# Splitting the tail of an output projection over POOL, ACT and DVE in an encoder layer

## The chip, the cores and the metric

The kernel runs on one core of one Trainium2 chip. The metric is the device time of one execution in microseconds (us), lower is better. The engines are named as in the profile: PE (TensorE, matrix products and transposes), DVE (VectorE), ACT (ScalarE), POOL (GpSimd) and SP (SyncE, which here only issues transfers). Each engine takes its own instructions in program order; between engines only semaphores set an order.

## The reference

One layer of a bidirectional encoder with adaLN conditioning is applied to two groups of tokens, 256 "prompt" and 1024 "sample" tokens of width 1024, that share all weights. All inputs and outputs are float32. Per layer:

```
h  = RMSNorm(x) * (1 + scale1) + shift1
q, k, v, gates of two attention branches = h @ w_in
x  = x + gate1 * ((sigmoid(gA) * oA + sigmoid(gB) * oB) @ w_out)
h2 = RMSNorm(x) * (1 + scale2) + shift2
aff = softmax(h2 @ w_router); each of 16 experts takes its top 2n/16 tokens
x  = x + gate2 * (weighted sum of expert SwiGLU outputs)
y  = RMSNorm(x)
```

The case is about the third to fifth line: the residual, the second norm and its modulation by scale2 and shift2, and the router behind them. The modulated h2 is transposed (features on partitions), so scale and shift are one number per partition there. The experts' token lists need the router values of all tokens of a group.

## The kernel before

The 1280 tokens are 10 tiles of 128 (NT = 10; tiles 0 and 1 are the prompt). `plan_steps` writes out one list of steps by hand, and every engine walks through this same list and issues its own part of each step. For the stage in question the list is a loop over t from 0 to 12, and each pass holds, in this order:

- `O` t: PE multiplies tile t of the merged attention output with w_out, 48 products of 128 x 512 in bf16 into two PSUM banks (lines 1376 to 1378). It waits for `out_free`, so that the banks of two tiles before are read.
- `X2` t-1: PE transposes the normalised tile `xn2` in two halves of four transposes (line 1431) and DVE modulates each transposed 128 x 128 block (`modulate`, line 1029), eight per tile, into `h2T`.
- `RT` t-2: PE computes the router logits of a tile in 16 products (line 1591), DVE takes the row maximum (line 1236), ACT the exponential (line 945), DVE reciprocal and scaling (lines 1238 and 1239).
- `AT` t-3: PE transposes the affinities (line 1597), DVE copies them out (line 1247).
- `K` 0, in pass 6 only: DVE picks the prompt's top tokens (`topk`, lines 1037 to 1044).
- `XO` t: DVE waits for `out_done` and multiplies the projection in PSUM with gate1 (line 1225), adds the residual `xo` (line 1227), waits for ACT's sum of squares (line 939), scales it (1019), waits for ACT's square root (941), takes the reciprocal (1021) and scales the rows into `xn2` (1229). POOL then stores `xn2` and `x1` to DRAM (lines 672 and 673).

Behind the loop come the diagonals of gate2 (`GT` 4 to 7, lines 1205 and 1529), the sample group's top 128 tokens (`K` 1, 48 long DVE instructions), the transposes of the lists (`I`), and then the gather of the first expert's tokens and the experts. `XO` t is the last step of pass t, while the transposes that read its `xn2` are in pass t+1, behind the products of tile t+1. ACT's square root and its exponential need different tables, so that a table load (`ACT_TABLE_LOAD`) stands before each of them.

The ring of three PSUM banks for transposes (`job_at`, `t_free`) is freed by whoever read a bank. Line numbers below are those of the printed kernel.

Of the kernel before, what the change touches and what calls it, by code (L numbers as in the profile page):

```python
# [19 lines left out]
ALU = mybir.AluOpType  # L20
ACT = mybir.ActivationFunctionType
AX = mybir.AxisListType

P = 128
D = 1024
# [3 lines left out]
NT = TOK // P  # L29
# [12 lines left out]
EPS = 1e-6  # L42
# [33 lines left out]
def group_of(t):  # L76
    return 0 if t < PT_TILES else 1
# [120 lines left out]
def encoder(nc, x_p, x_s, c_p, c_s, w_ada, b_ada, n1g, w_in, qg, kg, sink, w_ba, w_bb, w_out, n2g, w_router,  # L198
# [25 lines left out]
    with ExitStack() as ctx:  # L224
# [3 lines left out]
        def sem(name):  # L228
            return ctx.enter_context(nc.semaphore(name))
# [62 lines left out]
        xo = at(12288, 2, D)  # L292
        x1 = at(14336, 2, D)
        xn2 = at(16384, 2, D)
        h2T = [at(18432, KD, P), at(46592, KD, P)]
# [24 lines left out]
        modT = sb("modT", [P, 48, 2])  # L320
        A1 = sb("A1", [P, KD, 2])
        A2 = sb("A2", [P, KD, 2])
# [9 lines left out]
        rs = sb("rs", [P, 2, 8])  # L332
# [33 lines left out]
        ssq = sem("ssq")  # L366
        rms_in, rms_sqrt = sem("rms_in"), sem("rms_sqrt")
# [11 lines left out]
        msum, mhigh = sem("msum"), sem("mhigh")  # L379
        wos_hi, wos_ready = sem("wos_hi"), sem("wos_ready")  # L380
        out_done, out_free = sem("out_done"), sem("out_free")
        xo_in = [sem("xo_in0"), sem("xo_in1")]
        x1_ready, xn2_ready = sem("x1_ready"), sem("xn2_ready")
        x1_out, xn2_out = [sem("x1_out0"), sem("x1_out1")], [sem("xn2_out0"), sem("xn2_out1")]
# [226 lines left out]
        def _(gp):  # L611
# [12 lines left out]
            for s in steps:  # L624
                k = s[0]
                if k == "RB":
                    g = s[1]
                    if g:
                        gp.wait_ge(t_done, job_at[(("OT", g - 1), 0)] + 1)
                    if NPAIR * g == first_b:  # L630
                        gp.wait_ge(pv_done, first_b)
                    gp.wait_ge(rinv_ready, g + 1)
                    gp.tensor_tensor(rb_of(g).rearrange("p (h d) -> p h d", d=HD),  # L633
                                     ones[:, 0:HD].unsqueeze(1).to_broadcast([P, 8, HD]),
                                     rinv[:, g % 2].unsqueeze(2).to_broadcast([P, 8, HD]), ALU.mult).then_inc(rb_ready, 1)
                if k == "NM":
                    g = s[1]
                    br, _, qt, _ = items[NPAIR * g]
                    o = oT[:, NPAIR * br:NPAIR * br + NPAIR, qt]
                    src = on_of(g).rearrange("p (j q) -> p j q", j=NPAIR)  # L640
                    gp.wait_ge(o_norm, g + 1)
                    gp.tensor_tensor(o[:, :, 0:P], src, ones[:, 0:NPAIR].unsqueeze(2).to_broadcast([P, NPAIR, P]), ALU.mult)\
                        .then_inc(o_high, 1)
                    gp.wait_ge(o_high, g + 1)
                    gp.tensor_tensor(o[:, :, P:2 * P], src, o[:, :, 0:P], ALU.subtract).then_inc(o_split, 1)
                if k == "HS":

                    t = s[1]
                    if t == 0:
                        gp.wait_ge(t_done, job_at[(("AR", 11), 0)] + 1)  # L650
                        gp.wait_ge(pv_done, first_b)
                    a, z = t * P, t * P + P
                    gp.tensor_tensor(hTs[:, 0:KD, a:z], hT[:, :, a:z], ones[:, 0:KD].unsqueeze(2).to_broadcast([P, KD, P]),
                                     ALU.mult).then_inc(hs_hi, 1)
                    gp.wait_ge(hs_hi, t + 1)
                    gp.tensor_tensor(hTs[:, KD:2 * KD, a:z], hT[:, :, a:z], hTs[:, 0:KD, a:z], ALU.subtract).then_inc(hs_done, 1)
                if k == "M":
                    n = (s[1] * 3 + s[2])
                    w = 256 if s[2] == 2 else 512
                    gp.wait_ge(mm_ready, n + 1)  # L660
                    tmp = sig[:, n % 2, 0, 0:w]
                    cols = slice(s[2] * 512, s[2] * 512 + w)
                    gp.tensor_tensor(tmp, tmp, sig[:, n % 2, 1, 0:w], ALU.add).then_inc(msum, 1)  # L663
                    gp.wait_ge(msum, n + 1)
                    gp.tensor_tensor(mergedS[:, s[1], cols], tmp, ones[:, 0:1].to_broadcast([P, w]), ALU.mult).then_inc(mhigh, 1)
                    gp.wait_ge(mhigh, n + 1)
                    gp.tensor_tensor(mergedS[:, KD + s[1], cols], tmp, mergedS[:, s[1], cols], ALU.subtract)\
                        .then_inc(merged_ready, 1)
                if k in ("XO",):
                    t = s[1]  # L670
                    gp.wait_ge(xn2_ready, t + 1)
                    gp.dma_start(token_rows(xn_d, t), xn2[:, t % 2]).then_inc(xn2_out[t % 2], 16)
                    gp.dma_start(token_rows(acc_d, t), x1[:, t % 2]).then_inc(x1_out[t % 2], 16)
# [96 lines left out]
        def _(ac):  # L770
# [23 lines left out]
            for s in steps:  # L794
                k = s[0]
                if k == "vec":
                    b, free = job(s)
# [4 lines left out]
                if k == "br":  # L802
                    b, free = job(s)

                    ac.activation(brow[:, s[1], :], b[:, 0:RELW], ACT.Copy).then_inc(brow_ready, 1)
                if k == "AR":
                    c = s[1]
                    b, free = job(s)
# [4 lines left out]
                if k == "XP":  # L813
                    t = s[1]
# [7 lines left out]
                if k == "G":  # L822
                    t = s[1]
# [4 lines left out]
                    for c in range(3):  # L828
                        ac.wait_ge(g_done, 3 * t + c + 1)
                        n = 3 * t + c  # L830
                        b = ps[:, n % 5]
# [6 lines left out]
                        if c == 0:  # L838
                            ins = ac.activation(raw[:, 0:512], b, ACT.Copy)
# [8 lines left out]
                if k == "N":  # L848
                    t = s[1]
                    ac.wait_ge(q_in, t + 1)  # L850
                    ac.activation(qs[:, 2], qs[:, 1], ACT.Sqrt).then_inc(q_sqrt, 1)
                if k == "Q":
                    t = s[1]
# [4 lines left out]
                if k == "OT":  # L858
                    g = s[1]
# [73 lines left out]
                if k == "XO":  # L933
                    t = s[1]
                    ac.wait_ge(x1_ready, t + 1)
                    if t >= 2:
                        ac.wait_ge(t_done, job_at[(("X2", t - 2), 1)] + 1)
                        ac.wait_ge(xn2_out[t % 2], 16 * (t // 2))
                    ac.activation(xn2[:, t % 2], x1[:, t % 2], ACT.Square, accum_out=rs[:, t % 2, 0:1]).then_inc(ssq, 1)
                    ac.wait_ge(rms_in, NT + t + 1)  # L940
                    ac.activation(rs[:, t % 2, 2:3], rs[:, t % 2, 1:2], ACT.Sqrt).then_inc(rms_sqrt, 1)
                if k == "RT":
                    t = s[1]
                    ac.wait_ge(rmax, t + 1)
                    ac.activation(lg[:, t % 2], ps[:, 4, 0:NE], ACT.Exp, bias=rst[:, t % 2, 0:1],
                                  accum_out=rst[:, t % 2, 1:2]).then_inc(rexp, 1)
# [48 lines left out]
        def _(ve):  # L995
# [8 lines left out]
            def job(s, n=0):  # L1004
                j = job_at[(s, n)]
                ve.wait_ge(t_done, j + 1)
                return ps[:, bank_of(j)], t_free[j % 3]
# [7 lines left out]
            def norm_in(n):  # L1015

                ve.wait_ge(ssq, n + 1)
                t = n % NT
                ve.tensor_scalar(rs[:, t % 2, 1:2], rs[:, t % 2, 0:1], 1.0 / D, EPS, ALU.mult, ALU.add).then_inc(rms_in, 1)
                ve.wait_ge(rms_sqrt, n + 1)  # L1020
                link(ve.reciprocal(rs[:, t % 2, 3:4], rs[:, t % 2, 2:3]))

            def modulate(s, dst, A, sh, g):

                for half in range(2):
                    b, free = job(s, half)
                    for q in range(4):
                        kk = half * 4 + q
                        ins = ve.tensor_scalar(dst(kk), b[:, q * P:(q + 1) * P], A[:, kk, g:g + 1],  # L1029
                                               modT[:, sh + kk, g:g + 1], ALU.mult, ALU.add)  # L1030
                    ins.then_inc(free, 1)
# [24 lines left out]
            for s in steps:  # L1056
# [158 lines left out]
                if k == "XO":  # L1215
                    t = s[1]
                    g = group_of(t)
                    if t == 0:
                        ve.wait_ge(gt_ready, 4)
                    ve.wait_ge(out_done, t + 1)  # L1220
                    ve.wait_ge(xo_in[t % 2], 16 * (t // 2 + 1))
                    if t >= 2:
                        ve.wait_ge(x1_out[t % 2], 16 * (t // 2))
                    o = ps[:, 2 * (t % 2):2 * (t % 2) + 2].rearrange("p a b -> p (a b)")
                    ve.tensor_tensor(x1[:, t % 2], o, gt1b[:, g], ALU.mult).then_inc(out_free, 1)
                    ve.wait_ge(out_free, t + 1)
                    ve.tensor_tensor(x1[:, t % 2], x1[:, t % 2], xo[:, t % 2], ALU.add).then_inc(x1_ready, 1)
                    norm_in(NT + t)
                    ve.tensor_scalar(xn2[:, t % 2], x1[:, t % 2], rs[:, t % 2, 3:4], None, ALU.mult).then_inc(xn2_ready, 1)
                if k == "X2":  # L1230
                    t = s[1]
                    modulate(s, lambda kk: h2T[t % 2][:, kk, :], A2, 24, group_of(t))
                if k == "RT":
                    t = s[1]
                    ve.wait_ge(r_done, t + 1)
# [487 lines left out]
```

## Time and profile before

| | us |
|---|---|
| median of 3 runs | 2605.61 (2605.5 to 2606.56) |
| the profiled execution, its own time | 2605.64 |
| its span in the profile | 2603.8 |
| pass 5 of the stage, start of transposes to start of transposes | 1067.24 to 1080.29 |
| the stage's last transposes start at | 1138.40 |
| the sample group's top-k on DVE | 1155.17 to 1215.1 |
| first expert product (line 1376) | 1231.83 |
| busy shares of the span: PE, DVE, ACT, POOL | 92%, 62%, 44%, 43% |

Times in the rows are from the span's start. In a timeline row the columns are start, duration, engine, line, operation, output<-input with shapes, and how many such instructions the row merges; the brackets give how long the engine was idle before it and who released it. PE's records of products that follow each other overlap: their starts tell the rate, not their lengths. The columns of the other views stand at their first group.

### The profile page before, as it was taken

The numbers are of one execution on the slowest core, as the hardware profiler recorded it, in microseconds if no ns is written. First come the engines' busy times: TensorE is split into PE (matmuls) and PEld (weight loads), VectorE is DVE, ScalarE is ACT, GpSimd is POOL, SyncE is SP. The second block draws the span as 40 slices with busy tenths as digits, with TensorE's granted clock in tenths as the row PEclk, the third lists the DMA queues.
The fourth block names the chain that finished last, engine by engine and source line by source line (L and its number), as shares of the span: only waits on it lengthen the run. The fifth ranks groups of instructions, "written<-read, shape, count | busy, mean of one in ns | idle before, by whom it ended". The sixth has DMA issues, their size and how long they took to land.

```text
span 2603.8 us, 53873 instructions
## 1 busy us (share of the span) xinstructions
PE 2389.2 (92%) x23508; PEld 1713.2 (66%) x23508; DVE 1611.2 (62%) x2022; ACT 1157.8 (44%) x1458; POOL 1125.8 (43%) x721
## 2 busy tenths in 40 slices
PE   6999899998899999951899999999999999999993
PEld 2444467655555555541888888888888888888872
DVE  1444366546211115557688788887888788887872
ACT  2111255556311113231556655665555655555552
POOL 0000011137232321024465677766767667776640
PEclk8999899999999999975999999999999999999997
DMA  8000300130211202243589989999899998999965
GB/s 318 17 24 0 113 1 2 66 130 1 81 30 44 49 33 83 104 171 131 205 324 333 319 314 334 332 321 320 313 333 328 325 318 322 327 335 320 315 240 188
DMA packets 230113, 512.23 MB, mean 197 GB/s; under 512 B 7819, under 2 KB 35580, under 8 KB 229756
## 3 DMA queue, kind: packets, MB, share of 16 engines
q1 hardware_dynamic: 219324, 477.36, 51.5%
q0 software_dynamic: 10560, 31.46, 4.4%
q8 instruction: 186, 3.05, 0.5%
q14 instruction: 43, 0.35, 0.0%
HBM read 480.49 MB, written 28.31 MB: 195 GB/s over the span
## 4 chain that ended last, share of the span: by engine, by line
PE 85%; DVE 7%; ACT 2%; DMA 2%; issue 2%; SPq 1%; POOL 1%; DVEq 0%; ACTq 0%; POOLq 0%
PE ps L1376 20%; PE ps L1377 20%; PE ps L1378 20%; PE ps L1445 8%; PE ps L1654 3%; PE ps L1499 3%; PE ps L1511 3%; PE ps L1480 3%; DVE arena L1029 1%; DVE ti_s L1038 1%; ACT arena L875 1%; DVE top_s L1037 1%; DVE arena L1039 1%; PE ps L1591 1%; PE ps L1490 1%
## 5 line engine op out<-in xcount | busy, mean ns | idle before, releaser
L1376 PE MATMUL ps<-arena 128*128 128x160 bf16 (+2 forms) x5344 | 1309.5, 264 | 21.8 <-DVE arena L1308 8.2
L1377 PE MATMUL ps<-arena 128*128 128x160 bf16 (+2 forms) x5344 | 1309.8, 264 | 0.0
L1378 PE MATMUL ps<-arena 128*128 128x160 bf16 (+2 forms) x5344 | 1309.3, 264 | 0.0
L1275 DVE TENSOR_TENSOR arena<-arena 128x2048 bf16<-128x2048 f32 x376 | 921.2, 2455 | 186.5 <-ACT arena L780 185.8
L780 ACT ACTIVATE arena<-arena 128x2048 bf16<-128x2048 f32 x384 | 726.8, 1904 | 237.0 <-PE ps L1378 179.2
L1376 PEld LDWEIGHTS ps<-arena 128*128 128x128 bf16 x5344 | 524.4, 98 | 155.1 <-issue 27.5
L1378 PEld LDWEIGHTS ps<-arena 128*128 128x128 bf16 x5344 | 524.5, 98 | 128.2 <-issue 2.5
L1377 PEld LDWEIGHTS ps<-arena 128*128 128x128 bf16 x5344 | 524.5, 98 | 119.2 <-issue 1.9
L704 POOL TENSOR_TENSOR arena<-arena 128x320 bf16<-128x320 f32 x128 | 282.0, 2203 | 10.0
L701 POOL TENSOR_TENSOR arena<-arena,ones 128x320 bf16<-128x320 f32 x128 | 181.7, 1419 | 183.5 <-DVE arena L1308 183.2
L966 ACT ACTIVATE arena<-ps 128x160 f32<-128x160 f32 x256 | 77.6, 304 | 354.4 <-PE ps L1378 352.2
L1445 PE MATMUL ps<-arena 128*128 128x512 f32 x480 | 210.3, 598 | 15.9 <-DMA arena<-w_in 15.9
L633 POOL TENSOR_TENSOR arena<-ones,rinv 128x512 f32<-128x512 f32 x20 | 20.9, 1044 | 416.9 <-DVE rinv L1179 360.1
L1213 DVE TENSOR_TENSOR arena<-arena,ps 128x512 f32<-128x512 f32 (+1 forms) x48 | 26.6, 595 | 247.7 <-ACT arena L931 247.7
L1445 PEld LDWEIGHTS ps<-arena 128*128 128x128 f32 x480 | 91.4, 192 | 127.8 <-issue 127.8
L931 ACT ACTIVATE arena<-ps 128x512 f32<-128x512 f32 (+1 forms) x48 | 22.6, 523 | 264.7 <-PE ps L1378 264.7
L1499 PE MATMUL ps<-ident,arena 128*128 128x128 f32 x752 | 113.6, 285 | 20.1 <-ACT arena L886 17.6
L1499 PEld LDWEIGHTS ps<-ident,arena 128*128 128x128 f32 x752 | 81.3, 143 | 75.8 <-issue 44.8
L1029 DVE TENSOR_SCALAR arena<-ps,A,modT 128x128 f32<-128x128 f32 x160 | 52.8, 403 | 111.5 <-PE ps L1431 111.4
L663 POOL TENSOR_TENSOR arena<-arena 128x512 f32<-128x512 f32 (+1 forms) x24 | 26.1, 1087 | 219.0 <-DVE arena L1213 219.0
L690 POOL TENSOR_TENSOR arena<-arena,ones 128x480 bf16<-128x480 f32 (+1 forms) x48 | 101.4, 2113 | 39.8 <-DVE arena L1267 39.8
L1308 DVE TENSOR_TENSOR arena<-arena,ps 128x160 f32<-128x160 f32 x256 | 79.5, 311 | 61.0 <-POOL arena L704 43.9
(194 smaller groups left out, 2339.0 us busy)
## 6 DMA issues: line engine op xcount, KB each, us to landing
arena<-w_e_gate SPq DMA_DIRECT2D x64, 2048.0 KB
arena<-w_e_up SPq DMA_DIRECT2D x64, 2048.0 KB, 9.3
arena<-w_e_down SPq DMA_DIRECT2D x64, 2048.0 KB, 9.1
arena<-w_ada SPq DMA_DIRECT2D x12, 2048.0 KB, 8.0
arena<-x_sample SPq DMA_DIRECT2D x16, 512.0 KB, 3.5
arena<-w_in SPq DMA_DIRECT2D x16, 512.0 KB, 5.1
arena<-w_in SPq DMA_DIRECT2D x3, 2048.0 KB, 16.8
arena<-w_out SPq DMA_DIRECT2D x2, 2048.0 KB, 7.9
```

The source lines that it names most:

```text
L690: gp.tensor_tensor(xeT[par][:, 0, d0:d1], src, ones[:, 0:d1 - d0].unsqueeze(2).to_broadcast([P, d1 - d0, SLOTS]), ALU.mult).then_inc(high, 1)
L701: gp.tensor_tensor(hidT[par][:, 0, f:f + 2], src, ones[:, 0:2].unsqueeze(2).to_broadcast([P, 2, SLOTS]), ALU.mult).then_inc(high, 1)
L704: gp.tensor_tensor(hidT[par][:, 1, f:f + 2], src, hidT[par][:, 0, f:f + 2], ALU.subtract).then_inc(hid_done, 1)
L780: ac.activation(split_half(slot, a)[0], stage_half(kind, a), ACT.Copy).then_inc(hi_done, 1)
L1029: ins = ve.tensor_scalar(dst(kk), b[:, q * P:(q + 1) * P], A[:, kk, g:g + 1], modT[:, sh + kk, g:g + 1], ALU.mult, ALU.add)
L1275: ve.tensor_tensor(lo, stage_half(kind, a), hi, ALU.subtract).then_inc(lo_done, 1)
L1308: ve.tensor_tensor(hid32[:, f % 4], sil[:, f % 2], ps[:, f % 3, SLOTS:2 * SLOTS], ALU.mult)\
L1376: pe.matmul(out, w_hi, x_hi, start=start, stop=False)
L1377: pe.matmul(out, w_hi, x_lo, start=False, stop=False)
L1378: return pe.matmul(out, w_lo, x_hi, start=False, stop=stop)
L1445: ins = pe.matmul(ps[:, n % 5], hT[:, kk, t * P:(t + 1) * P], wqkv[c][:, kk, :], start=(kk == 0), stop=(kk == KD - 1))
L1499: ins = pe.transpose(b[:, q * P:(q + 1) * P], probs(i, hh)[:, (a + q) * P:(a + q + 1) * P], ident[:])
```

## The change

The changed kernel divides step `XO` and step `X2` differently.

- DVE's multiplication with gate1 stays, but no longer waits for the residual. The addition of the residual moves to POOL, in place in `x1`, behind waits for `out_free` and the residual's load.
- DVE still computes the mean square and the reciprocal, and now signals `r2_ready`.
- ACT, behind its square root, waits for `r2_ready` and scales the rows with a `Copy` whose scale is that reciprocal, one number per partition.
- Of the eight blocks of `X2`, DVE keeps the first half (`halves=1`). ACT does the second with `Identity`, with scale and bias as one number per partition each.

```
                 if k in ("XO",):                                   # POOL
                     t = s[1]
+                    gp.wait_ge(out_free, t + 1)
+                    gp.wait_ge(xo_in[t % 2], 16 * (t // 2 + 1))
+                    gp.tensor_tensor(x1[:, t % 2], x1[:, t % 2], xo[:, t % 2], ALU.add).then_inc(x1_ready, 1)
                     gp.wait_ge(xn2_ready, t + 1)
...
                     ac.activation(rs[:, t % 2, 2:3], rs[:, t % 2, 1:2], ACT.Sqrt).then_inc(rms_sqrt, 1)
+                    ac.wait_ge(r2_ready, t + 1)
+                    ac.activation(xn2[:, t % 2], x1[:, t % 2], ACT.Copy, scale=rs[:, t % 2, 3:4]).then_inc(xn2_ready, 1)
+                if k == "X2":
+                    t = s[1]
+                    g = group_of(t)
+                    b, free = job(s, 1)
+                    for q in range(4):
+                        ins = ac.activation(h2T[t % 2][:, 4 + q, :], b[:, q * P:(q + 1) * P], ACT.Identity,
+                                            scale=A2[:, 4 + q, g:g + 1], bias=modT[:, 28 + q, g:g + 1])
+                    ins.then_inc(free, 1)
...
                     ve.wait_ge(out_done, t + 1)
-                    ve.wait_ge(xo_in[t % 2], 16 * (t // 2 + 1))
...
                     ve.tensor_tensor(x1[:, t % 2], o, gt1b[:, g], ALU.mult).then_inc(out_free, 1)
-                    ve.wait_ge(out_free, t + 1)
-                    ve.tensor_tensor(x1[:, t % 2], x1[:, t % 2], xo[:, t % 2], ALU.add).then_inc(x1_ready, 1)
-                    norm_in(NT + t)
-                    ve.tensor_scalar(xn2[:, t % 2], x1[:, t % 2], rs[:, t % 2, 3:4], None, ALU.mult).then_inc(xn2_ready, 1)
+                    ve.wait_ge(ssq, NT + t + 1)
+                    ve.tensor_scalar(rs[:, t % 2, 1:2], rs[:, t % 2, 0:1], 1.0 / D, EPS, ALU.mult, ALU.add).then_inc(rms_in, 1)
+                    ve.wait_ge(rms_sqrt, NT + t + 1)
+                    ve.reciprocal(rs[:, t % 2, 3:4], rs[:, t % 2, 2:3]).then_inc(r2_ready, 1)
                 if k == "X2":
                     t = s[1]
-                    modulate(s, lambda kk: h2T[t % 2][:, kk, :], A2, 24, group_of(t))
+                    modulate(s, lambda kk: h2T[t % 2][:, kk, :], A2, 24, group_of(t), halves=1)
```

ACT's instructions of one pass of the loop before: the squares of `XO` (L939), the square root with its table (L941), the exponential of `RT` with its table (L945).

```order
L939 ACTIVATE arena,rs<-arena 128x1024
L941 ACT_TABLE_LOAD
L941 ACTIVATE rs<-rs 128x1
L945 ACT_TABLE_LOAD
L945 ACTIVATE lg,rst<-ps,rst 128x16
```

And now, with the changed kernel's line numbers: squares (L943), square root (L945), the row scaling (L947), the second half of the next tile's modulation (L953), the exponential (L959).

```order
L943 ACTIVATE arena,rs<-arena 128x1024
L945 ACT_TABLE_LOAD
L945 ACTIVATE rs<-rs 128x1
L947 ACTIVATE arena<-arena,rs 128x1024
L953 ACTIVATE arena<-ps,modT,A 128x128 x4
L959 ACT_TABLE_LOAD
L959 ACTIVATE lg,rst<-ps,rst 128x16
```

There are as many table loads as before; the exponential's load moved from right behind the square root to behind the four modulating instructions, which themselves wait for PE's transposes.

DVE's instructions of one pass before, from the modulation (L1029) over the router's softmax (L1236 to L1239) and the copy of the affinities (L1247) to `XO` (L1225 to L1229):

```order
L1029 TENSOR_SCALAR arena<-ps,A,modT 128x128 x8
L1236 TENSOR_REDUCE rst<-ps 128x1
L1238 RECIPROCAL rst<-rst 128x1
L1239 TENSOR_SCALAR af<-lg,rst 128x16
L1247 COPY yeP<-ps 16x128
L1249 ISA
L1225 TENSOR_TENSOR arena<-ps,arena 128x1024
L1227 TENSOR_TENSOR arena<-arena 128x1024
L1019 TENSOR_SCALAR rs<-rs 128x1
L1021 RECIPROCAL rs<-rs 128x1
L1229 TENSOR_SCALAR arena<-arena,rs 128x1024
```

And now, the same pieces (L1043, L1249 to L1252, L1260, L1238 to L1242):

```order
L1043 TENSOR_SCALAR arena<-ps,A,modT 128x128 x4
L1249 TENSOR_REDUCE rst<-ps 128x1
L1251 RECIPROCAL rst<-rst 128x1
L1252 TENSOR_SCALAR af<-lg,rst 128x16
L1260 COPY yeP<-ps 16x128
L1262 ISA
L1238 TENSOR_TENSOR arena<-ps,arena 128x1024
L1240 TENSOR_SCALAR rs<-rs 128x1
L1242 RECIPROCAL rs<-rs 128x1
```

DVE lost four modulating instructions and the two 128 x 1024 instructions behind the gate's multiplication; the order of the rest is as it was. On POOL an addition of 128 x 1024 stands ahead of the two stores of each tile. PE's and SP's instructions are the same.

## Rows read from the trace of the kernel before

**Rows 1.** Windows: start:end, length, busy us per engine, PEclk, DMA share, GB/s.
```profile
1071.00:1084.00 13.00, 13.00 (x74) 7.42 (x73) 6.83 (x17) 4.24 (x8) 1.06 (x2) 1.00 0.33 121
```

**Rows 2.** Timeline of PE: transposes and router products of some passes, products after the first stall.
```profile
1067.24 1.04 PE L1431 MATMUL ps<-ident,arena 128*128 128x128 f32 x8
1068.11 1.86 PE L1591 MATMUL ps<-wr,arena 128*128 128x16 f32 x16
...
1080.29 1.04 PE L1431 MATMUL ps<-ident,arena 128*128 128x128 f32 x8
...
1097.28 1.97 PE L1431 MATMUL ps<-ident,arena 128*128 128x128 f32 x8 [3.79 <-DVE arena L1229]
1102.48 0.63 PE L1376 MATMUL ps<-arena 128*128 128x512 bf16 x1
...
1138.40 1.97 PE L1431 MATMUL ps<-ident,arena 128*128 128x128 f32 x8 [7.92 <-DVE arena L1229]
```

**Rows 3.** Timeline of DVE, pass 5.
```profile
1067.88 2.64 DVE L1029 TENSOR_SCALAR arena<-ps,A,modT 128x128 f32<-128x128 f32 x8 [2.96 <-PE ps L1431]
1070.44 0.17 DVE L1236 TENSOR_REDUCE rst<-ps 128x1 f32<-128x16 f32 x1
...
1071.80 1.23 DVE L1225 TENSOR_TENSOR arena<-ps,arena 128x1024 f32<-128x1024 f32 x1
1073.06 1.23 DVE L1227 TENSOR_TENSOR arena<-arena 128x1024 f32<-128x1024 f32 x1
...
1077.01 0.16 DVE L1021 RECIPROCAL rs<-rs 128x1 f32<-128x1 f32 x1 [1.36 <-ACT rs L941]
1077.21 0.75 DVE L1229 TENSOR_SCALAR arena<-arena,rs 128x1024 f32<-128x1024 f32 x1
```

**Rows 4.** Timeline of ACT, pass 5.
```profile
1070.64 0.27 ACT L945 ACTIVATE lg<-ps,rst 128x16 f32<-128x16 f32 x1 [5.41 <-DVE rst L1236]
1070.81 0.19 ACT L945 ACTIVATION_READ_ACCUMULATOR lg<-ps,rst 128x1 f32 x1
1074.31 1.06 ACT L939 ACTIVATE arena<-arena 128x1024 f32<-128x1024 f32 x1 [3.31 <-DVE arena L1227]
...
1076.77 0.20 ACT L941 ACTIVATE rs<-rs 128x1 f32<-128x1 f32 x1
1076.99 1.28 ACT L945 ACT_TABLE_LOAD   x1
```

**Rows 5.** Timeline of DVE, pass 6, around the prompt's top-k.
```profile
1084.43 0.27 DVE L1247 COPY arena<-ps 16x128 f32<-16x128 f32 x1
...
1091.06 1.23 DVE L1225 TENSOR_TENSOR arena<-ps,arena 128x1024 f32<-128x1024 f32 x1
```

**Rows 6.** Groups of POOL by line and shape: busy us, mean ns | idle before.
```profile
L656 POOL TENSOR_TENSOR arena<-arena 128x1024 bf16<-128x1024 f32 x10 | 21.3, 2132 | 0.8
...
L663 POOL TENSOR_TENSOR arena<-arena 128x512 f32<-128x512 f32 x16 | 20.3, 1269 | 189.8 <-DVE arena L1213 189.8
...
L663 POOL TENSOR_TENSOR arena<-arena 128x256 f32<-128x256 f32 x8 | 5.8, 724 | 29.2 <-DVE arena L1213 29.2
```

**Rows 7.** Timeline of DVE and POOL, a hand-over from one to the other.
```profile
983.04 1.28 DVE L1213 TENSOR_TENSOR arena<-arena,ps 128x512 f32<-128x512 f32 x2 [14.26 <-ACT arena L931]
984.40 1.27 POOL L663 TENSOR_TENSOR arena<-arena 128x512 f32<-128x512 f32 x1 [11.92 <-DVE arena L1213]
```

**Rows 8.** Groups of ACT by line and shape.
```profile
L875 ACT ACTIVATE arena<-ps,nm 128x1024 f32<-128x1024 f32 x64 | 71.3, 1115 | 5.0 <-DVE nm L1152 3.1
...
L819 ACT ACTIVATE arena<-arena 128x1024 f32<-128x1024 f32 x10 | 10.4, 1042 | 26.1 <-DMA arena<-x_sample 26.1
...
L836 ACT ACTIVATE arena<-ps 128x128 f32<-128x128 f32 x20 | 5.8, 289 | 12.4 <-PE ps L1445 12.4
...
L945 ACT ACTIVATE lg<-ps,rst 128x16 f32<-128x16 f32 x10 | 2.7, 274 | 55.3 <-DVE rst L1236 55.3
```

**Rows 9.** Window after the first stall: PEclk.
```profile
1106.00:1107.00 1.00, 1.00 (x6) 0.44 (x5) 0.36 (x1) 0.60 (x1) 0.00 (x0) 1.00 0.00 0
```

More of the change, by code:

```diff
@@ L381, in encoder @@
         out_done, out_free = sem("out_done"), sem("out_free")
+        r2_ready = sem("r2_ready")
         xo_in = [sem("xo_in0"), sem("xo_in1")]
@@ L1021, in norm_in, with modulate @@
                 link(ve.reciprocal(rs[:, t % 2, 3:4], rs[:, t % 2, 2:3]))
-            def modulate(s, dst, A, sh, g):
-                for half in range(2):
+            def modulate(s, dst, A, sh, g, halves=2):
+                for half in range(halves):
                     b, free = job(s, half)
```

## The prediction

> **What bounds the kernel now.** I read the windows by stretch first, since they say which engine is full where. In pass 5 of the stage PE is busy for the whole 13.0 us at full clock, while DVE works 6.83, ACT 4.24 and POOL 1.06 us of it [rows 1]. PE's timeline says the same: transposes start at 1067.24 and again at 1080.29, and nobody released them, so a round of PE takes 13.05 us and everything else fits into it [rows 2]. The engines that the change relieves and loads are therefore hidden in these passes, as long as their own round stays below 13.05 us.
>
> The same timeline shows two places where PE does wait for the row scaling of DVE (line 1229): before the transposes of tile 6, 3.79 us, and before those of tile 9, 7.92 us [rows 2]. The first follows the prompt's top-k, which stands between 1084.43 and 1091.06 on DVE in front of `XO` 6 [rows 5]. The second is the end of the stage: no products are left behind which `XO` 9 could hide. From there a serial chain over the router, the sample group's top-k and the gather leads into the experts, so a delay of tile 9 is a delay of the end. So the question is only how long the chain from one tile's transposes to the next tile's `xn2` becomes, twice exposed, and whether it outgrows PE's round elsewhere.
>
> **That chain before, in pass 5**, counted from T = 1067.24, when the transposes of tile 4 start. They end at T + 1.04 [rows 2]. DVE modulates to about T + 3.28, takes the maximum at T + 3.20, ACT's exponential starts at T + 3.40 [rows 3, 4]. The gate's multiplication starts 1.16 later (1071.80 less 1070.64), the squares 2.51 after that (1074.31 less 1071.80), the reciprocal 2.70 after the squares, and it takes 0.16. From its end to the end of the row scaling it is 0.04 + 0.75, and 0.06 more until PE starts in the exposed place [rows 2 to 4]. Sum: 3.40 + 1.16 + 2.51 + 2.86 + 0.85 = 10.78 us, 2.27 us under PE's round.
>
> **The change, part by part.**
>
> *The modulation, half of it on ACT.* DVE is relieved of four of eight blocks, 1.32 us (half of 2.64). This is worth little, since the maximum needs the router's products too, which PE ends at 1068.11 + 1.86, T + 2.73 [rows 2]. ACT is what gets longer: the exponential's table load stood right behind the square root, long before it was needed (1076.99), and the exponential then waited 5.41 us [rows 4]. Now the load stands behind four `Identity` instructions, which can't start before the second half of the transposes, T + 1.07 with 0.03 for the hand-over (1074.31 against the end 1074.28 of DVE's addition). No row has an `Identity` with scale and bias from memory. With one such operand, 1024 columns cost 1115 ns and 16 columns 274 ns, 0.834 ns a column, so 128 columns cost 0.367 us; without one they cost 0.289 us [rows 8]. One operand is then 0.078 us, and two make 0.445 us. Instructions of ACT overlap by 0.10 us (the accumulator's read starts 0.17 into a 0.27 us instruction [rows 4]). Four take 3 x 0.345 + 0.445 = 1.48 us; the bounds are 4 x 0.289 = 1.16 and 4 x 0.445 = 1.78. They end at T + 2.55, the load ends at T + 3.85, the exponential starts at T + 3.86: 0.46 us later than before (0.14 to 0.76).
>
> *The residual on POOL.* Before, multiplication start to squares start was 2.51 us. Now it is 1.23 us, a hand-over to POOL of 0.08 us (983.04 + 1.28 against 984.40 [rows 7]), POOL's addition, and a hand-over to ACT. For the addition the nearest rows are of the same types and half the width: 1269 ns for 512, 724 ns for 256, so 2.13 ns a column and 1.27 + 512 x 0.00213 = 2.36 us for 1024. The row of the right width but with a bf16 operand has 2.13, twice the 512 row is 2.54; these are the bounds [rows 6]. I take the same types. DVE waits in that time, so nothing competes with POOL. For the hand-over to ACT I take 0.10; from both sides 0.03 to 0.3, since no row has it. Sum 1.23 + 0.08 + 2.36 + 0.10 = 3.77 us, 1.26 us more (0.9 to 1.7).
>
> A rule of the Trainium skill stands against this part ("GPSIMD Engine Reference", Engine selection): elementwise work with two inputs belongs on VectorE, GpSimd being about twice slower. Its figure of 4497 ns for 2048 columns gives an estimate of 2.25 us for our addition; by it the total below would be 2609.6 instead of 2609.8.
>
> *The row scaling on ACT.* 0.75 us on DVE [rows 3] becomes a `Copy` over 1024 columns with one operand from memory: 1.04 us without [rows 8], plus 0.078, 1.12 us (1.04 to 1.20). That is 0.37 us more, and no hand-over more, since the reciprocal's result went through a semaphore before as well.
>
> *Stores, loads, waits.* POOL's two stores of tile t were behind the row scaling and still are; the next use of these buffers is two tiles later, some 20 us. The load of the residual for tile t+2 waits for `x1_ready`, 1.26 us later, and is not needed for two passes. DVE no longer waits for the residual. Behind POOL's new waits only its own stores are queued. None of this is on the path. The bank of the second half is freed by ACT at T + 2.55, earlier than DVE did.
>
> **The sum.** Per exposed chain 0.46 + 1.26 + 0.37 = 2.09 us. At the first place it delays PE by 2.09, since the top-k starts behind the exponential and copy of its pass as before and keeps its length. PE then runs a full pass at lower clock in which DVE and ACT have time over, and `XO` 7 and 8 are hidden again. At the second place 2.09 us more come on top. What follows there, the router of tiles 8 and 9, is slow on PE (transposes take 1.97 us [rows 2]), so ACT's four instructions and the load, 2.8 us, end before the maximum is there and cost nothing. In the other passes the chain grows to 3.86 + 1.16 + 3.77 + 2.86 + 1.22 = 12.87 us, still 0.18 us under PE's 13.05. Together 2605.64 + 4.18 = 2609.8 us, against the profiled execution's own time; the median of the runs before differs from it by 0.03 us, so nothing is corrected. The span would be about 2608.0.
>
> **Unknown at the first place.** The transposes restart at 1097.28 at half clock (1.97 against 1.04 us), and the dense products from 1102.48 still run at 0.63 us; full clock is back at 1106 [rows 2, 9]. Those 3.6 us at half clock with dense work cost 1.8 us. A wait that is 2 us longer may shift where the clock returns, so I allow 1.8 us either way.
>
> **The rivals.** *The round opens.* The margin of 0.18 us is smaller than the bounds: with all of them at the upper end the chain is 12.87 + 0.30 + 0.4 + 0.08 = 13.65 us, and PE waits 0.6 us in each pass where the chain has the exponential and the affinities' copy (before the transposes of tiles 3, 4, 5 and 8). It decides as soon as the chain passes 13.05 us. With half of that, 0.3 x 4 = 1.2 on PE and 2 x 0.48 in the exposed chains, the time is 2612.0; at the full ends 2.4 + 1.6, 2613.8. This is the case that is clearly slower. For it: a thin margin made of unseen durations. Against it: each estimate is from near rows, and DVE's start after the copy may win a tenth.
>
> *The load costs more where it stands now.* Before, the load begins 0.02 us behind a short square root [rows 4]. Behind four back-to-back instructions it might need ACT to run empty first, at most, I'd say, another load's length of 1.28. Then each exposed chain grows by that and four rounds open by 12.87 + 1.28 - 13.05 = 1.10: 2609.8 + 2.56 + 4.4 = 2616.8. The rows speak against it: the load at 1076.99 starts as soon as ACT is free. The Trainium skill ("ScalarE: Activation LUTs", What ACT_TABLE_LOAD costs) has this as a rule, about 1.38 us of drain with each switch; by it the time would be 2617.4, and the trace, with 0.02 us before each load, does not agree.
>
> *Hardly a change.* If ACT's four instructions, the addition and the hand-over are at the low ends, a chain grows by 1.36, 2.7 in all; if the clock also comes back 1.8 us of time sooner, the time is 2606.5. For it: the relieved DVE, the overlap on ACT. A gain would need PE's round or the top-k to get shorter, and no instruction of either is touched: the relief of DVE lies beside PE's work.
>
> **Chances.** The forecast 0.58 with its own range 2608.0 to 2611.5; the round opens 0.24; the load 0.03; hardly a change 0.15. A measurement of this kernel can tell about 0.2%, 5.2 us. Above 2610.8 lie the upper part of the forecast (0.10), nearly all of the opened round (0.21) and the load (0.03), with 0.01 unforeseen: 0.35. Faster than 2600.4 only by something that I don't see, 0.03. The range 2607.2 to 2613.2 leaves out the load, the far ends of the opened round and of the cheap case.
>
> **What would show it.** PE's transposes of tile 6 should start at about 1099.4 with 5.9 us idle, those of tile 9 at about 1142.6 with 10.0 us; POOL's addition near 2.36 us, the row scaling on ACT 1.12, four `Identity` 1.48, the exponential 3.86 us behind the transposes' start. No idle time of PE before the other tiles' transposes. PE waiting there means that the round opened. A total under 2605 would mean that the chain was not what PE waited for.

## The result and the profile after

The changed kernel takes 2610.78 us (median of 20 runs, 2608.04 to 2613.71), the kernel before 2605.23 us in the runs beside it (20 runs, 2603.19 to 2607.50): ratio 1.0022, 95% interval 1.0015 to 1.0029, or 5.6 us slower. The forecast was 2609.8 with a range of 2607.2 to 2613.2. The slowdown is clear, and its size lies on the bound of 0.2% that the prediction named.

The profiled execution after took 2610.12 us, span 2608.3. Its timeline is 1.0 us late already at the stage's first transposes (1017.98 against 1016.98); a second trace of each kernel has 1017.35 and 1015.50 there, so this much comes and goes with the trace. So below, times are compared as distances from that point.

The timeline of PE after, at the tiles that the prediction spoke of; line 1444 is the line 1431 of before, to be read against [rows 2].

```profile
1100.29 1.97 PE L1444 MATMUL ps<-ident,arena 128*128 128x128 f32 x8 [5.80 <-ACT arena L947]
...
1118.31 1.04 PE L1444 MATMUL ps<-ident,arena 128*128 128x128 f32 x8
...
1131.45 1.09 PE L1444 MATMUL ps<-ident,arena 128*128 128x128 f32 x8
...
1144.30 1.97 PE L1444 MATMUL ps<-ident,arena 128*128 128x128 f32 x8 [9.95 <-ACT arena L947]
```

The waits at tiles 6 and 9 grew from 3.79 and 7.92 to 5.80 and 9.95 us, and who ends them is now ACT's row scaling. No other tile's transposes have a wait in brackets. From the first transposes of the stage to those of tile 9 it is 126.32 us, 121.42 before (1138.40 less 1016.98): 4.90 us more, of which the two waits explain 4.04.

The same pass as in [rows 3, 4], now the one whose transposes start at 1068.24. First ACT, with the exponential at line 959, the squares at 943, the row scaling at 947 and the modulation at 953:

```profile
1069.32 1.50 ACT L953 ACTIVATE arena<-ps,modT,A 128x128 f32<-128x128 f32 x4 [1.37 <-PE ps L1444]
1070.84 1.28 ACT L959 ACT_TABLE_LOAD   x1
1072.13 0.27 ACT L959 ACTIVATE lg<-ps,rst 128x16 f32<-128x16 f32 x1
...
1076.94 1.06 ACT L943 ACTIVATE arena<-arena 128x1024 f32<-128x1024 f32 x1 [4.45 <-POOL arena L674]
...
1079.84 1.15 ACT L947 ACTIVATE arena<-arena,rs 128x1024 f32<-128x1024 f32 x1 [0.23 <-DVE rs L1242]
```

DVE in that pass (maximum, gate's multiplication, reciprocal), and POOL's addition:

```profile
1071.01 0.17 DVE L1249 TENSOR_REDUCE rst<-ps 128x1 f32<-128x16 f32 x1 [0.76 <-PE ps L1604]
...
1073.26 1.23 DVE L1238 TENSOR_TENSOR arena<-ps,arena 128x1024 f32<-128x1024 f32 x1
...
1079.64 0.16 DVE L1242 RECIPROCAL rs<-rs 128x1 f32<-128x1 f32 x1 [1.36 <-ACT rs L945]
```

```profile
1074.57 2.34 POOL L674 TENSOR_TENSOR arena<-arena 128x1024 f32<-128x1024 f32 x1 [5.24 <-DVE arena L1238]
```

The reader is to see the reversal on ACT: before, the exponential waited 5.41 us for DVE's maximum [rows 4]. Now its row has no bracket, so ACT was not idle in front of it. The maximum is ready at 1071.18, and the exponential starts at 1072.13, as soon as its table is there. The table is loaded behind four instructions that themselves waited for PE.

Of the other 0.86 us, 0.15 is around tile 8 (its transposes come 13.14 us behind tile 7's, 13.04 before, and take 0.05 us longer); 0.71 is the clock. Windows of before around the first stall (the column with 1.00 or 0.50 is PEclk, 1.00 for 2.4 GHz and 0.50 for 1.2 GHz):

```profile
1095.00:1096.00 1.00, 0.00 (x0) 0.00 (x0) 0.00 (x0) 1.00 (x1) 0.00 (x0) 0.88 0.90 365
...
1104.00:1105.00 1.00, 1.00 (x3) 0.30 (x2) 1.00 (x1) 0.00 (x0) 0.00 (x0) 0.50 0.00 0
```

and of after:

```profile
1096.00:1097.00 1.00, 0.00 (x0) 0.00 (x0) 0.00 (x0) 0.80 (x1) 0.16 (x1) 0.90 0.00 0
1109.00:1110.00 1.00, 1.00 (x4) 0.36 (x3) 0.00 (x0) 0.00 (x0) 1.00 (x1) 0.50 0.00 0
1110.00:1111.00 1.00, 1.00 (x5) 0.38 (x4) 0.00 (x0) 0.46 (x1) 0.51 (x1) 0.77 0.00 0
```

Before, the clock is low from 1095.8 to 1106.0, 10.2 us; after, from 1096.8 to 1110.5, 13.7 us. It falls at the same distance from the stage's start (78.8 us in both), during the wait, but returns 3.4 us later, while the wait ended only 2.0 us later. So PE works at the low clock for 10.2 us behind the transposes of tile 6 instead of 8.7 (1100.29 to 1110.45, before 1097.28 to 1106.01). Half of the difference is lost: the pass from tile 6's to tile 7's transposes takes 18.02 us instead of 17.31.

### The profile page after: what moved, and what is told of

Read it like the earlier page. It is cut to its first block, busy times and chain, and to the rows that moved or that the text cites. A ratio compares the mean times of both kernels' runs of the same rounds, so it can differ in the third digit from the quotient of the medians.

```text
span 2608.3 us, 53882 instructions
## 1 busy us (share of the span) xinstructions
PE 2388.8 (92%) x23508; PEld 1713.0 (66%) x23508; DVE 1580.2 (61%) x1962; ACT 1183.8 (45%) x1508; POOL 1153.8 (44%) x731
## 4 chain that ended last, share of the span: by engine, by line
PE 86%; DVE 7%; ACT 2%; DMA 2%; issue 1%; SPq 1%; POOL 1%; DVEq 0%; ACTq 0%; POOLq 0%
PE ps L1389 20%; PE ps L1390 20%; PE ps L1391 20%; PE ps L1458 8%; PE ps L1667 3%; PE ps L1512 3%; PE ps L1524 3%; PE ps L1493 3%; ACT arena L879 1%; DVE ti_s L1052 1%; DVE top_s L1051 1%; DVE arena L1053 1%; DVE arena L1043 1%; PE ps L1604 1%; PE ps L1503 1%
## 5 line engine op out<-in xcount | busy, mean ns | idle before, releaser
L890 ACT ACTIVATE arena<-ps 128x512 f32<-128x512 f32 (+2 forms) x152 | 71.7, 498 | 83.3 <-PE ps L1512 83.2
```

## The experiments

All compare with the kernel before on the same chip. The table gives them as one; the lengths are from the traces: waits of PE before the transposes of tiles 6 and 9, length of the low clock around the first (from windows of 1 us, a window at PEclk 0.50 counting in full), the pass from tile 6's to tile 7's transposes, and S, from the stage's first transposes to DVE's first product of 128 x 160 in the experts.

| kernel | ratio (95%) | wait 6 | wait 9 | low clock | pass 7 | S |
|---|---|---|---|---|---|---|
| before | | 3.79 | 7.92 | 10.2 | 17.31 | 220.6 |
| c1, before again | one run | 3.79 | 7.93 | 10.2 | 17.19 | 220.3 |
| changed | 1.0022 (1.0015 to 1.0029) | 5.80 | 9.95 | 13.7 | 18.02 | 226.5 |
| c2, changed again | one run | 5.80 | 9.94 | 13.6 | 17.92 | 226.4 |
| e1, addition on POOL | 1.0011 (1.0002 to 1.0020) | 4.91 | 9.06 | 13.7 | 18.36 | 223.7 |
| e2, row scaling on ACT | 1.0002 (0.9992 to 1.0011) | 4.17 | 8.31 | 10.2 | 17.03 | 220.9 |
| e3, half modulation on ACT | 1.0001 (0.9991 to 1.0010) | 4.28 | 8.42 | 10.2 | 17.01 | 221.0 |
| e4, changed, slower POOL | 1.0039 (1.0024 to 1.0054) | 6.79 | 10.94 | 10.2 | 17.20 | 231.1 |
| e5, changed, ACT's half late | 1.0009 (1.0000 to 1.0018) | 4.89 | 9.03 | 13.7 | 18.36 | 223.7 |
| e6, before, ACT's half late | 0.9996 (0.9987 to 1.0005) | 3.35 | 7.50 | 10.2 | 17.49 | 220.2 |
| e7, before, top-k cut | 0.9975 (0.9966 to 0.9984) | none | 7.93 | none | 13.05 | 213.1 |
| e8, changed, top-k cut | 0.9977 (0.9966 to 0.9987) | none | 9.94 | none | 13.05 | 214.2 |
| e9, e6 with top-k cut | 0.9969 (0.9957 to 0.9982) | none | 7.50 | none | 13.05 | 212.9 |

**e1 to e3: one part at a time, in the kernel before.**

```
e1  POOL, XO:  + gp.wait_ge(out_free, t + 1); gp.wait_ge(xo_in[t % 2], ...)
               + gp.tensor_tensor(x1[:, t % 2], x1[:, t % 2], xo[:, t % 2], ALU.add).then_inc(x1_ready, 1)
    DVE, XO:   - ve.wait_ge(xo_in[t % 2], ...); - the addition and its wait
e2  ACT, XO:   + ac.activation(xn2[:, t % 2], x1[:, t % 2], ACT.Copy, scale=rs[:, t % 2, 3:4]).then_inc(xn2_ready, 1)
    DVE, XO:   - ve.tensor_scalar(xn2[:, t % 2], ...)
e3  ACT, X2:   + four ac.activation(..., ACT.Identity, scale=A2[...], bias=modT[...]) ahead of RT
    DVE, X2:   modulate(..., halves=1)
```

Expected of e1: 

> The kernel before with the first part alone: the residual is added by POOL, DVE keeps the row scaling and all eight modulating instructions. Theory (only the chain from one tile's transposes to the next tile's normalised rows counts, and only where PE waits for it): an addition of 2.34 us and two hand-overs in place of 1.23 us lengthen it by 1.25 us; PE waits 5.0 us before the transposes of tile 6 (3.79 before) and 9.2 us before those of tile 9 (7.92), nowhere else; time +2.5 us, ratio 1.0010. Rival (the whole slowdown comes from POOL, by the clock or by what POOL's work does to others): +4 us or more with these waits.

Measured: PE's timeline in e1 at tile 6, with its wait in brackets:

```profile
1097.74 1.97 PE L1431 MATMUL ps<-ident,arena 128*128 128x128 f32 x8 [4.91 <-DVE arena L1229]
```

and in the groups of the stage POOL's addition against DVE's:

```profile
L673 POOL TENSOR_TENSOR arena<-arena 128x1024 f32<-128x1024 f32 x10 | 23.4, 2339 | 69.2 <-DVE arena L1227 69.2
```

The waits grew by 1.12 and 1.14 us, 0.1 us less than expected, and the time by 3.0 us (0.5 to 5.2 by the interval, which excludes neither the theory's 2.5 nor the rival's 4). The trace decides: the transposes of tile 9 come 3.32 us later than before, counted from the stage's start. The waits give 2.26 of it, and nearly all of the rest, 1.05, is the clock, which stays low for 13.7 us as in the changed kernel (pass 7 takes 18.36 us, 17.31 before). The rival is wrong that the whole slowdown comes from POOL (3.32 of 4.90 us), but right that POOL's part costs more than its waits.

Expected of e2: 

> The kernel before with the second part alone: ACT scales the rows with a Copy, POOL and the modulation are as before. Theory: 1.15 us in place of 0.75, PE waits 4.2 us before tile 6 and 8.3 us before tile 9; +0.8 us in time, too small for the timing (ratio 1.000 to 1.001). Rival (ACT's queue is the trouble): clearly longer waits than these.

Expected of e3: 

> The kernel before with the third part alone: ACT modulates the second half of each tile ahead of the router's exponential. Theory: the exponential's table load ends behind four instructions of 1.5 us in all, the exponential starts 0.49 us later than before, PE waits 4.3 us before tile 6 and 8.4 us before tile 9; +1.0 us in time. Rival (half of the modulation off DVE pays): the waits get shorter by up to 0.4 us.

Measured: e2's waits grew by 0.38 and 0.39 us, e3's by 0.49 and 0.50. Both times are as before within their intervals; the 0.8 and 1.0 us expected were too small to be told from nothing there. ACT's rows in e3, in the pass whose transposes start at 1066.40:

```profile
1067.48 1.50 ACT L947 ACTIVATE arena<-ps,modT,A 128x128 f32<-128x128 f32 x4 [3.89 <-PE ps L1439]
1069.00 1.28 ACT L953 ACT_TABLE_LOAD   x1
1070.29 0.27 ACT L953 ACTIVATE lg<-ps,rst 128x16 f32<-128x16 f32 x1
```

The exponential is 3.89 us behind the transposes' start, 3.40 before [rows 2, 4]. The relief of DVE does not show, against e3's rival. The three parts add up: 1.12 + 0.38 + 0.49 = 1.99 at tile 6 and 1.14 + 0.39 + 0.50 = 2.03 at tile 9, against 2.01 and 2.03 in the changed kernel. For the waits the parts do not interact.

**c1 and c2: second traces.**

Expected of c1: 

> The kernel before, unchanged, for a second trace of it. If the place of the clock's return after the stall at tile 6 is a matter of chance, it differs between this trace and the first (8.8 us behind the transposes' start there, 9.9 in the changed kernel); if the length of the stall sets it, it is 8.8 again.

Expected of c2: 

> The changed kernel again, for a second trace. If the length of the wait sets where the clock returns behind tile 6, the low stretch is 13.7 us again (10.2 in both traces of the kernel before, 13.7 in the kernel with POOL's addition alone) and the pass behind it 18.0 us; if it is chance, it may be 10.2.

Measured: 10.2 us of low clock in both traces of before, 13.7 and 13.6 in both of the changed kernel, the waits the same to 0.01 us. The clock returned 8.5 us behind the transposes' start in c1 and 8.7 in the first trace. For these two kernels the low stretch is not chance from run to run. In the ten rows of the table that have one it has just two lengths, 10.2 and 13.7 us.

What this costs comes out exactly. In all ten rows pass 7 takes 12.9 us and half of the time for which the clock is still low behind the transposes of tile 6. That time is 8.1 to 9.1 us with the short stretch, and 10.0 to 10.9 with the long one. Within one length a longer wait makes the pass shorter, since less of the stretch is left when PE restarts (17.31, 17.03 and 17.01 us for waits of 3.79, 4.17 and 4.28); from the short to the long stretch half of 3.4 us, 1.7, is added.

Which length comes does not follow from the wait alone: 10.2 us up to a wait of 4.28, 13.7 from 4.89 to 5.80, and 10.2 again at 6.79 (e4). The ten rows fall in line when they are sorted by how long before the end of the wait the clock fell: 1.2 to 2.1 us in the six rows with the short stretch (e6, before, e4, c1, e2, e3), 2.8 to 3.7 in the four with the long one (e1, e5, changed, c2). In nine of them the clock falls 78.5 to 78.8 us from the stage's start, so that there a longer wait leaves more time behind the fall. In e4 it falls only 5.1 us into the wait, 1.7 before its end:

```profile
1101.00:1102.00 1.00, 0.00 (x0) 0.00 (x0) 0.00 (x0) 1.00 (x1) 0.00 (x0) 1.00 0.87 340
1102.00:1103.00 1.00, 0.00 (x0) 0.00 (x0) 0.16 (x1) 0.76 (x3) 0.00 (x0) 0.51 0.35 139
```

```profile
1103.75 1.97 PE L1445 MATMUL ps<-ident,arena 128*128 128x128 f32 x8 [6.79 <-ACT arena L948]
```

So c1's and c2's idea that the length of the wait sets the stretch holds for these two kernels, but not across all. Why the clock fell where it did in e4 is not shown, and the order by the fall was found in the finished traces: no run was made to test it.

**e4: is the thin margin real?**

```
+ gp.tensor_tensor(at(B + 12032, 512), xo[:, t % 2, 0:512], xo[:, t % 2, 0:512], ALU.add)
  gp.tensor_tensor(x1[:, t % 2], x1[:, t % 2], xo[:, t % 2], ALU.add).then_inc(x1_ready, 1)
```

Expected: 

> The changed kernel with one more POOL instruction of 512 columns (1.27 us, its result goes to free space and is not used) ahead of each residual addition. Theory (a round of 13.05 us on PE hides the chain; the changed kernel's chain is 0.3 us under it): the chain passes the round, PE waits about 1.0 us before the transposes of tiles 3, 4 and 5, 0.7 before tile 2, 1.3 before tile 8, and the two old waits grow to 7.1 and 11.2 us; the stage gets 6 to 8 us longer than in the changed kernel, time about +12 us over before (ratio 1.0045). Rival (only the two exposed places ever count): the old waits grow by 1.3 us each and nothing else, +2.6 us over the changed kernel, ratio 1.003.

Measured: the added instruction, whose two inputs are the same columns, took 1.03 us, not 1.27. PE's timeline, tiles 2, 3 and 5:

```profile
1041.28 1.09 PE L1445 MATMUL ps<-ident,arena 128*128 128x128 f32 x8 [0.30 <-ACT arena L948]
1055.13 1.09 PE L1445 MATMUL ps<-ident,arena 128*128 128x128 f32 x8 [0.58 <-ACT arena L948]
1083.69 1.09 PE L1445 MATMUL ps<-ident,arena 128*128 128x128 f32 x8 [0.58 <-ACT arena L948]
```

Tile 8 waits 0.94 us. The new waits are there, so the round opens as the theory says. Each is about 0.4 us under its forecast, of which the shorter instruction explains 0.24. Tile 4 has no wait, and that is the surprise: 2.5 us behind the end of the wait at tile 3 the clock fell.

```profile
1057.00:1058.00 1.00, 1.00 (x10) 0.98 (x10) 0.19 (x1) 0.98 (x4) 0.00 (x0) 0.83 0.91 348
1058.00:1059.00 1.00, 1.00 (x5) 0.41 (x3) 0.17 (x1) 1.00 (x1) 0.00 (x0) 0.50 1.02 414
1060.00:1061.00 1.00, 1.00 (x3) 0.30 (x2) 0.89 (x2) 0.00 (x0) 0.00 (x0) 0.50 0.00 0
1061.00:1062.00 1.00, 1.00 (x6) 0.50 (x5) 0.42 (x1) 0.00 (x0) 0.49 (x1) 0.97 0.00 0
```

For 3.4 us PE worked at half clock though it was busy, and the pass took 14.77 us instead of 13.05, long enough to hide the chain again. The wait alone does not bring this about: the same 0.58 us before tile 5 and the 0.94 us before tile 8 had no such fall behind them. What sets tile 3 apart is open. The transposes of tile 9 come 5.97 us later than in the changed kernel. The old waits account for 0.99 each. Of the other 3.99 us, the new waits are 2.40 and the slow pass 1.72, while pass 7 is 0.82 shorter (its low stretch is the short one); 0.69 is spread over the passes. Forecast were 6 to 8 us and a time 12 us over before; by the medians it is 9.9 over. The rival (only the old waits, ratio 1.003) falls by the trace; the timing alone (1.0024 to 1.0054) would not have excluded it.

**e5 and e6: ACT's half behind the exponential.** The four `Identity` instructions stand behind the exponential of the same pass, and for tile 9 ahead of it.

```
  if k == "RT" ...:
      ac.wait_ge(rmax, t + 1)
      ac.activation(lg[:, t % 2], ps[:, 4, 0:NE], ACT.Exp, ...).then_inc(rexp, 1)
+     four ac.activation(h2T[...], b[...], ACT.Identity, scale=..., bias=...) of tile t + 1
```

Expected of e5: 

> The changed kernel with ACT's four modulating instructions of a tile behind the exponential of the same pass instead of ahead of it (ahead only for the last tile, where the next router products wait for them). Theory: the exponential's table load hides again behind the row scaling, the exponential starts 3.0 us behind the transposes' start instead of 3.9 (3.4 in the kernel before), PE waits 4.9 us before tile 6 and 9.0 before tile 9, the clock behind tile 6 returns as in the kernel with POOL's addition alone; +3 us over before. Rival (the relief of DVE never shows): the waits stay at 5.8 and 9.95 us.

Expected of e6: 

> The kernel before with ACT modulating the second half of each tile behind the exponential; addition and row scaling stay on DVE. Theory: here the relief of DVE reaches the chain, since the maximum no longer stands behind eight modulating instructions: the exponential starts 0.4 us earlier, PE waits 3.4 and 7.5 us, time -0.8 us, in the noise (ratio 0.999 to 1.000). Rival: no change of the waits.

Measured in e5, in the pass with transposes at 1066.29, and below it in e6, with transposes at 1068.38:

```profile
1065.09 1.28 ACT L952 ACT_TABLE_LOAD   x1
1069.27 0.27 ACT L952 ACTIVATE lg<-ps,rst 128x16 f32<-128x16 f32 x1 [2.90 <-DVE rst L1257]
...
1069.53 1.50 ACT L961 ACTIVATE arena<-ps,modT,A 128x128 f32<-128x128 f32 x4
```

```profile
1071.35 0.27 ACT L946 ACTIVATE lg<-ps,rst 128x16 f32<-128x16 f32 x1 [5.41 <-DVE rst L1252]
...
1071.61 1.49 ACT L955 ACTIVATE arena<-ps,modT,A 128x128 f32<-128x128 f32 x4
```

The exponential starts 2.98 and 2.97 us behind the transposes, the waits are those expected to 0.05 us. One position in ACT's order is worth 0.91 us per exposed place. The part of the change that moved the modulation is thus not bad in itself: with the exponential first it shortens the waits of before by 0.44 and 0.42 us. In time e6's 0.9996 is not told from 1.

**e7 to e9: away with the first exposed place.** The experiments before say that the change costs where PE waits, and the larger waste is that PE waits there at all. The prompt's top-k has four turns in a row, each working on what the one before left of the values; they have to stay in this order, but need not stand in one piece ahead of `XO` 6.

```
-        if t == 6:
-            s.append(("K", 0))
         if t < NT:
             s.append(("XO", t))
+        if 4 <= t < 8:
+            s.append(("KP", t - 4))      # one turn of topk(0, affP)
```

Expected of e7: 

> The kernel before with the prompt's top-k cut into its four turns of eight, one behind XO in each of passes 4 to 7 (before: all four ahead of XO in pass 6). Theory: a turn of 1.35 us fits into the 3 us in which DVE idles there, the wait of 3.8 us before tile 6 and the low clock behind it are gone, only the wait of 7.9 us at tile 9 stays: 8.2 us less, 2597.4, ratio 0.9969. Rival: PE waits elsewhere for the turns, gain under 4 us.

Expected of e8: 

> The same cut of the top-k in the changed kernel. Theory: the first exposed place is gone, with it 2.0 us of the change's cost and all of the clock's part; what is left over e7 is 2.0 us at tile 9 (wait 9.9), and nothing at tiles 2 to 8 (their margin is 0.3 us): ratio to before 0.9977. Rival (the turns on DVE delay the modulation and use up the thin margin): waits before tiles 5 to 8 and little gain.

Expected of e9: 

> The cut top-k with ACT modulating the second half behind the exponential, addition and row scaling on DVE: the two edits that shorten the chain. Theory: as e7 and 0.4 us less at tile 9 (wait 7.5), ratio 0.9967. Rival: nothing over e7.

Measured: a turn in e7 on DVE, between the row scaling and the next modulation:

```profile
1090.60 0.76 DVE L1231 TENSOR_SCALAR arena<-arena,rs 128x1024 f32<-128x1024 f32 x1
1091.27 0.41 DVE L1037 MAX8 top_p<-yeP 16x8 f32<-16x256 f32 x1
...
1092.18 0.40 DVE L1039 MATCH_REPLACE8 yeP<-top_p,yeP 16x256 f32<-16x256 f32 x1
1094.32 2.64 DVE L1029 TENSOR_SCALAR arena<-ps,A,modT 128x128 f32<-128x128 f32 x8 [1.74 <-PE ps L1435]
```

DVE still idles 1.74 us behind the turn, so nothing is late. The transposes of tile 9 start 8.20 us earlier than before from the stage's start (113.22 against 121.42), as expected. Less of it reaches the end: S is 7.5 us shorter, and the time 5.9 us by the medians (2599.41 against 2605.27), 4.2 to 8.9 by the interval of the ratio, where 8.2 was expected. In S 0.54 us is lost again behind the first expert product, where the clock returns later than before (told in the next section). PE's only wait before transposes of the stage, in e7 and in e8:

```profile
1130.47 1.97 PE L1435 MATMUL ps<-ident,arena 128*128 128x128 f32 x8 [7.93 <-DVE arena L1231]
```

```profile
1132.02 1.97 PE L1448 MATMUL ps<-ident,arena 128*128 128x128 f32 x8 [9.94 <-ACT arena L947]
```

In e8 the change's cost at tile 9 is there in full, 2.01 us, and at tiles 1 to 8 nothing: their passes are those of e7, 13.05 us each from tile 3 on. The rival of e8 falls. Later things blur the difference: it is 2.0 us up to the experts' first product and 1.1 in S, where the way from there to DVE's first product was 0.8 us shorter in e8's trace; the ratios of e7 and e8 can't be told apart. e9 has the shortest wait at tile 9 (7.50). Its median is 2597.57 us (6 runs) against 2605.27 before. All three beat the kernel before, by 6 to 8 us, and so the changed kernel, which lies 5.6 us above that; which of e7 and e9 is better their intervals don't say.

## Why the prediction was right

- *What bounds the kernel* held: PE's round hides the chain in all passes but two, and the waits at tiles 6 and 9 carry the change. Shown by e1 to e3 (the waits add up) and by e8 (without the first place only the second is left).
- *The exponential behind the moved table load*: forecast 0.46 us, measured 0.49 (e3). Four `Identity` took 1.50 us, forecast 1.48. The cause, the order on ACT, is shown by e5 and e6.
- *The addition on POOL*: 2.34 us, forecast 2.36; the hand-over to POOL 0.08 as forecast, that to ACT 0.03 where I took 0.10. From the multiplication's start to the squares' start it is 3.68 us, forecast 3.77; e1 measured 1.12 and 1.14 us, forecast 1.26.
- *The row scaling on ACT*: 1.15 us, forecast 1.12; e2 measured 0.38, forecast 0.37.
- *The sum of the two waits*: forecast 4.18, measured 4.04.
- *The margin of the other rounds*: forecast 0.18, measured 0.25. (The row scaling ends at 1067.94 and the transposes start at 1068.24, 0.30 later; the forecast's chain ends 0.06 behind the row scaling, with the hand-over to PE, which took 0.05 where PE waited.) e4 shows that it is a real edge. A small exception: tile 8's transposes came 13.14 us behind tile 7's. DVE's multiplication of `XO` 8 starts 0.47 us behind its copy there instead of about 0.1, in both traces of the changed kernel and in e5, but not in e1 or e8. The cause is open.
- *The term that was mis-sized* is the clock. The prediction allowed 1.8 us either way and put zero into the sum. It was a cost that came back: 0.71 us in pass 7 in the first trace, 0.73 in the second against the second of before. The prediction also counted half a microsecond of loss per microsecond for the dense products alone (from 1102.48 to 1106.0, which is 3.5 us and not 3.6). The transposes and the router's products are slowed as well: all of the 8.7 us at the low clock behind the restart cost half of themselves, 4.4 us in pass 7 before and 5.1 after.
- *Behind the stage.* In the first trace another 0.92 us came behind the first expert product, again at half clock (from there to DVE's first product 6.71 us, 5.79 before; 6.63 and 5.84 in the second traces). In all thirteen traces this way takes 3.8 to 3.9 us and half of the time for which the clock is still low behind the first expert product (3.9 us before, 5.8 in the changed kernel). It does not grow with the delay: the other kernels have 5.31 to 6.60 us, e4 with the largest delay only 5.41. So it is part of this kernel's slowdown, but through where the clock returns, for which the prediction had no term; whether another kernel with the same delay would have it is open. Together with the waits, pass 7 and tile 8 it makes the 5.8 us in S, where the timing has 5.6.
- *What was luck.* The forecast of the added time, 4.2 us, is 1.4 short of the measured 5.6. The measured time lies inside the range since the range was wider than the waits alone needed, by the clock's 1.8 us and by the opened round; the clock's part in pass 7 and behind the stage (0.71 and 0.92 us) happened to stay within that.
- *The rivals.* The round did not open, but for the tenth at tile 8. The moved table load costs no more than its 1.28 us: the exponential starts 0.01 us behind its end (1070.84 + 1.28 against 1072.13). The drain that the Trainium skill adds to each load ("ScalarE: Activation LUTs", What ACT_TABLE_LOAD costs) is not seen here either. Its figure for GpSimd, from which I had estimated 2.25 us ("GPSIMD Engine Reference", Elementwise — side-by-side cycle accounting), was near the 2.34 measured, and its advice to keep such additions on VectorE holds here. The cheap case is out by the waits, which grew by 2.01 and 2.03 us where it had 1.36, and by the clock, which came back later and not sooner.

## What to carry to other kernels

Work is cheap on an idle engine only where the chain through it is hidden. The share of busy time (DVE 6.8, ACT 4.2 us in a round of 13) said nothing about the two places that counted, so find where the bounding engine waits and add up hand-overs there. A table load's place in ACT's order matters as well: behind other work that waits, it moves onto the path (0.91 us per exposed place, e5). And when a change makes a wait a little longer, ask first whether the wait could go: cutting the top-k that caused it gave about 6 us, as much as the whole change had cost.

## What the runs showed of the hardware

- The low clock around the wait at tile 6 came in two lengths only, 10.2 and 13.7 us, in ten traces. The pass behind it took 12.9 us and half of what was left of the low stretch when PE restarted. In nine of the traces the wait of 4.9 us had the longer stretch and that of 4.3 the shorter; e4, with 6.8 us and the short one, shows that the wait's length alone does not decide.
- The clock can fall in a pass in which PE idled for only 0.58 us, ahead of transposes and the router's thin products, and stay low for 3.4 us while PE is busy (e4, tile 3). It did not fall behind the same wait at tile 5 nor behind 0.94 us at tile 8. In the rounds of the kernel before, with the same instructions on PE and no wait, it stayed at 1.00 [rows 1].
- `Identity` with scale and bias from memory over 128 columns from PSUM took 456 ns, `Copy` with such a scale over 1024 columns 1148 ns (a `Square` of 1024 columns without one 1042 [rows 8]); an addition of 1024 float32 columns took 2.34 us on POOL and 1.23 us on DVE [rows 3].
